# Two transformer blocks on one core: the first weight block behind each adaLN norm multiplies rows not yet normed

## What is computed

```python
def rms_norm(x, g):
    return x * lax.rsqrt(jnp.mean(x * x, -1, keepdims=True) + EPS) * g
def modulate(x, m, i):                  # shift m[3i], scale m[3i+1], gate m[3i+2]
    return x * (1 + scale) + shift
m = jax.nn.silu(cond) @ w_mod + b_mod   # 9 * 1024 numbers for LAT and for CTX, per layer
for l in range(2):
    u = modulate(rms_norm(x, g0), m, 0)                      # norm n0_l
    x = x + 0.5 * m[2] * swiglu(u, ffn_w_in[l,0], ffn_w_out[l,0])     # up_l0, down_l0
    u = modulate(rms_norm(x, g1), m, 1)                      # norm n1_l
    p = u @ w_in[l]                                          # q_l, k_l, f_l, v_l, gates
    x = x + m[5] * (mixer(p) @ w_o[l])                       # w_o_l
    u = modulate(rms_norm(x, g2), m, 2)                      # norm n2_l
    x = x + 0.5 * m[8] * swiglu(u, ffn_w_in[l,1], ffn_w_out[l,1])     # up_l1, down_l1
```

## Time and profile before

| what | value |
|---|---|
| median of 3 runs | 2754.08 us (2753.29 to 2756.24) |
| the profiled execution, its own time | 2759.6 us |
| its span | 2757.8 us |
| mean granted PE clock | 0.978 of full |
| busy: PE, DVE, ACT, POOL | 96%, 51%, 37%, 48% |
| time in weight matmuls at L1615, share of the chain that ended last | 57% |

### The profile page before, as it was taken

The page is one execution under the profiler, slowest core; times in us unless marked ns, Lnnn a source line. Parts: engine busy times, 40 slices in busy tenths (PEclk is TensorE's granted clock), DMA queues, the critical chain, the costliest instruction groups (busy, mean ns, idle before and its releaser), DMA issues.

```text
span 2757.8 us, 42480 instructions
## 1 busy us (share of the span) xinstructions
PE 2634.6 (96%) x15112; PEld 2268.3 (82%) x15112; DVE 1395.3 (51%) x3037; ACT 1023.9 (37%) x1747; POOL 1312.6 (48%) x654
## 2 busy tenths in 40 slices
PE   7998989979999999999999999999999999998997
PEld 7968989978888878867787888878888878887997
DVE  3562765675544442355497444454455453647222
ACT  4345457442322132166513232232321232463542
POOL 4505858744443434133343444444443453455875
PEclk9999989989999999999999999999999999999999
DMA  5604635554443443121243443444443453324554
GB/s 191 222 24 154 213 121 184 176 159 153 148 136 112 125 148 122 39 85 46 77 148 128 144 144 113 120 130 156 137 132 115 148 169 100 100 93 138 168 164 124
DMA packets 413994, 365.71 MB, mean 133 GB/s; under 512 B 7484, under 2 KB 412558, under 8 KB 413888
## 3 DMA queue, kind: packets, MB, share of 16 engines
q1 hardware_dynamic: 411448, 359.14, 41.0%
q10 hardware_dynamic: 2440, 5.16, 0.5%
HBM read 363.19 MB, written 1.08 MB: 132 GB/s over the span
## 4 chain that ended last, share of the span: by engine, by line
PE 68%; issue 14%; POOL 12%; DVE 3%; ACT 2%; DMA 0%; POOLq 0%; SPq 0%; ACTq 0%; DVEq 0%
PE bank L1615 57%; POOL w_lo L655 12%; PE bank L2021 2%; PE bank L1675 1%; PE bank L1676 1%; PE bank L1680 1%; PE bank L2061 1%; PE bank L1625 1%; PE bank L1966 1%; DVE stat L1521 1%; PE bank L1767 1%; PE bank L1958 1%; PE bank L2047 0%; PE bank L1978 0%; DVE bank L1145 0%
## 5 line engine op out<-in xcount | busy, mean ns | idle before, releaser
L655 POOL TENSOR_TENSOR w_lo<-raw,w_hi 128x1024 fp32r<-128x1024 f32 (+2 forms) x602 | 1285.9, 2150 | 1343.9 <-ACT w_hi L726 936.2
L1615 PE MATMUL bank<-u_hi,w_hi 128*128 128x512 f32 (+1 forms) x2488 | 854.0, 343 | 2.8 <-POOL w_lo L655 2.8
L1615 PE MATMUL bank<-u_hi,w_lo 128*128 128x512 f32 (+1 forms) x2488 | 845.9, 340 | 0.0
L1615 PE MATMUL bank<-u_lo,w_hi 128*128 128x512 f32 (+1 forms) x2488 | 845.2, 340 | 0.0
L726 ACT ACTIVATE w_hi<-raw 128x1024 fp32r<-128x1024 f32 (+3 forms) x412 | 387.0, 954 | 985.7 <-PE bank L1615 794.3
L1615 PEld LDWEIGHTS bank<-u_hi,w_hi 128*128 128x128 f32 x2488 | 473.5, 190 | 74.8 <-issue 25.1
L1615 PEld LDWEIGHTS bank<-u_hi,w_lo 128*128 128x128 f32 x2488 | 473.6, 190 | 52.7
L1615 PEld LDWEIGHTS bank<-u_lo,w_hi 128*128 128x128 f32 x2488 | 473.7, 190 | 49.1
L1189 DVE SCALAR_TENSOR_TENSOR bank<-mod_raw,cond,bank 128x256 f32<-128x256 f32 x864 | 344.7, 481 | 1.4 <-DMA mod_raw<-in_w_mod 1.4
L1615 PE MATMUL bank<-hid_hi,w_hi 128*128 128x512 f32 (+1 forms) x880 | 309.8, 352 | 11.3 <-POOL w_lo L655 11.3
L1615 PE MATMUL bank<-hid_hi,w_lo 128*128 128x512 f32 (+1 forms) x880 | 307.0, 349 | 0.0
(11 more groups left out here) (239 smaller groups left out, 3387.2 us busy)
## 6 DMA issues: line engine op xcount, KB each, us to landing
raw<-in_ffn_w_in SPq DMA_DIRECT2D x88, 1024.0 KB, 5.1
mod_raw<-in_w_mod SPq DMA_DIRECT2D x144, 512.0 KB, 4.3
raw<-in_w_in SPq DMA_DIRECT2D x67, 1024.0 KB, 5.2
raw<-in_ffn_w_out SPq DMA_DIRECT2D x64, 704.0 KB, 4.6
raw<-in_w_ffn_up SPq DMA_DIRECT2D x22, 1024.0 KB, 5.1
raw<-in_w_ffn_down SPq DMA_DIRECT2D x16, 704.0 KB, 4.8
raw<-in_w_attn_out SPq DMA_DIRECT2D x8, 1024.0 KB, 5.2
raw<-in_w_o SPq DMA_DIRECT2D x8, 1024.0 KB, 5.2
```

The source lines that it names most:

```text
L655: pool.tensor_tensor(st.half(t, w_lo[slot]), st.half(t, raw[slot]), st.half(t, w_hi[slot]).bitcast(f32), ALU.subtract).then_inc(lo_ready, 1)
L1615: ins = pe.matmul(dst, s, v, start=first and n == 0, stop=final and n == 2)
```

## The change

- Each adaLN norm becomes a `late_norm`. The first weight block behind it (`n_late` = 1; for `n0_0` the first two) multiplies "early" rows x·mod_a, not divided by the root and without the shift. ACT makes their `u_hi` (`early_tiles`) and DVE their `u_lo` (`early_rest`) in the product ahead, as each tile of x is finished; for `n0_0`, CTX between the bodies of `down1` and LAT inside `n_ffn_post`.
- PE first multiplies the block with the shift itself, in two parts (`shifts`: 2 tiles x 8 k x 2 parts = 32 matmuls of 4 columns), then runs the block (`late_blocks`). The column sums come after its k = 0, the spread after k = 1 (k = 2 where it is 256 rows wide). ACT copies the result out, DVE multiplies it by the spread root (`scale`), ACT adds W·shift as a bias (`finish`).
- Meanwhile DVE and ACT form the normed rows, which overwrite `u_hi` and `u_lo` as PE frees each k (`u_free`). The second block runs k by k as they get ready, as the first did.
- ACT splits block 2 of the product between its passes, and `split_first` puts each weight split of the product ahead before the early tiles. `root` now takes the last tile too, and `column_sums` reads it alone (4 columns instead of 8).
- The 72 pairs of `w_mod` are dealt out anew: `down_00` and `down_01` carry two pairs per body (loads after blocks 1 and 3), `gates1_2` one, and body 0 of the four up products and of `q_0`, all of `w_o_0`, `q_1` and `f_1` none. `modulation(l, 2)` moves ahead of `w_o`, `modulation(0, 0)` between the bodies of `down1`; each makes `shift_parts` besides (one copy, one subtraction).

```diff
-        gemm(f"up_{l}0", pairs(a["ffn_w_in_2"][l, 0]), 22, mod=True, banks=(0, 1))
+        first = late_norm(f"n0_{l}", 1 if l else 2, early=KD if l else 2 * KD, summed=l > 0)
+        gemm(f"up_{l}0", pairs(a["ffn_w_in_2"][l, 0]), 22, mod=1, mod_bodies=range(1, 11), banks=(0, 1), **first)
         gemm(f"down_{l}0", down(a["ffn_w_out_2"][l, 0]), 16, per=4, kt=DOWN_KT, cols=P, banks=(0, 1),
-             mod=True, acc=2)
-        norm(f"n1_{l}", TO_U, summed=True, halves=2)
-        gemm(f"q_{l}", cols(w, 0), 4, mod=True)
-        gemm(f"k_{l}", cols(w, 1024), 4, mod=True)
+             mod=1 if last else 2, acc=2, whole=True)
+        first = late_norm(f"n1_{l}", 1, passes=2 * KD // halves)
+        gemm(f"q_{l}", cols(w, 0), 4, mod=0 if last else 1, mod_bodies=range(1, 2), **first)
+        gemm(f"k_{l}", cols(w, 1024), 4, mod=1)
         gemm(f"f_{l}", cols(w, 3072), 2, gpb=halves, banks=(0, 2) if last else (0, 1, 2, 3),
-             mod=True, token_major=True)
+             mod=0 if last else 1, token_major=True)
...
         plan.add(f"att_{l}", b3=units, unit=units, o=KD)
-        gemm(f"attn_out_{l}", cols(a["w_attn_out_2"][l], 0), 4, mod=not last, counted=False)
-        gemm(f"w_o_{l}", cols(a["w_o_2"][l], 0), 4, mod=not last, acc=4)
-        norm(f"n2_{l}", TO_U, summed=True, halves=halves)
-        gemm(f"up_{l}1", pairs(a["ffn_w_in_2"][l, 1]), 22, mod=not last, banks=(0, 1))
+        gemm(f"attn_out_{l}", cols(a["w_attn_out_2"][l], 0), 4, mod=0 if last else 1, counted=False)
+        gemm(f"w_o_{l}", cols(a["w_o_2"][l], 0), 4, acc=4, whole=True)
+        first = late_norm(f"n2_{l}", 1, halves=halves)
+        gemm(f"up_{l}1", pairs(a["ffn_w_in_2"][l, 1]), 22, mod=0 if last else 1, mod_bodies=range(1, 11),
+             banks=(0, 1), **first)
         gemm(f"down_{l}1", down(a["ffn_w_out_2"][l, 1]), 16, per=4, kt=DOWN_KT, cols=P, banks=(0, 1),
-             mod=not last, acc=2)
+             mod=0 if last else 2, acc=2, whole=not last)
...
+            def late_first(name, late_tile, func, w_sums, first=0, n_sums=1, extra=None, busy=None, evac=None):
...
+                def take(st, t):
+                    act.wait_ge(group_done, st.done(0, t + 1))
+                    if busy is not None:
+                        act.wait_ge(hid_prod, busy)
+                    dst = late_tile(t)
+                    act.activation(dst, bank[t][:, 0:S * len(late_halves(name))], ACT.Copy).then_inc(late_copied, 1)
+                def finish(t):
+                    act.wait_ge(scaled, sc0 + t + 1)
+                    dst = late_tile(t)
+                    for h in late_halves(name):
+                        ins = act.activation(dst[:, in_gemm(name, h)], dst[:, in_gemm(name, h)], func, bias=shift[:, t, h:h + 1])
+                    ins.then_inc(taken[t], 1)
+                def hi(st, n):
+                    k, halves = passes[n]
+                    act.wait_ge(xn_ready, x0 + sum(len(hs) for _, hs in passes[:n + 1]))
+                    if k < KD - 1:
+                        act.wait_ge(u_free, f0 + k + 1)
+                    else:
+                        act.wait_ge(group_done, st.done(0, 2 * st.n_late))
+                    for h in halves:
+                        ins = act.activation(u_hi[:, k, h * S:(h + 1) * S], normed(n)[:, in_norm(name, h)], ACT.Identity,
+                                             bias=mod[:, 3 * i_mod * KD + k, h:h + 1])
                     ins.then_inc(u_part, 1)
+                def emit(st, pick_table):
+                    mean_root(name, w_sums, n_sums, first)
+                    if extra is not None:
+                        extra()
+                    pick_table()
+                    if st.n_late == 2:
+                        for t in range(2):
+                            split_half(st, 0, t)
+                            take(st, t)
+                        for t in range(2):
+                            finish(t)
+                        for n in range(KD):
+                            hi(st, n)
+                        for t in range(2):
+                            split_half(st, 1, t)
+                            take(st, 2 + t)
+                        return
+                    for n in range(len(passes)):
+                        hi(st, n)
+                        if n in (3, 4):
+                            split_half(st, 0, n - 3)
+                        if n == 4:
+                            take(st, 0)
+                            take(st, 1)
+                        if n in (6, 7):
+                            finish(n - 6)
+                        if n == KD + 2:
+                            for t in range(2):
+                                split_half(st, 1, t)
+                    if len(passes) == KD:
+                        for t in range(2):
+                            split_half(st, 1, t)
+                    if evac is not None:
+                        for t in range(2, 4):
+                            evac(st, t)
...
+            def early_context():
+                act.wait_ge(gains_ready, 1)
+                for k in range(KD):
+                    early_tile(k, 0, [CTX])
+            gemm("down1", between=early_context)
             mean_root("n_ffn_post", S, 1)
+            act.wait_ge(diag_ready, plan.at("n0_0", "diag"))
+            act.activation(rms[:, 0, 0:S // P], ctx_rms[:, :], ACT.Copy).then_inc(ctx_ready, 1)
+            for k in range(KD):
+                act.wait_ge(updated, KD + k + 1)
+                early_tile(k, 0, [LAT])
+                act.activation(sq[:, k, :], x[:, k, S:T], ACT.Square).then_inc(sq_ready, 1)
...
+                gemm(f"up_{l}0", silu_tiles(T, base), table=ACT.Silu,
+                     first=late_first(f"n0_{l}", late_work(T), ACT.Silu, *sums, busy=base))
+                gemm(f"down_{l}0", early_tiles(f"n1_{l}", 2), split_first=True)
...
+            def early_rest(at, i, halves):
+                for h in halves:
+                    cols = slice(h * S, (h + 1) * S)
+                    by = mod_a[:, i, at, h:h + 1] if isinstance(at, int) else mod_a[:, i, at, h]
+                    ins = dve.scalar_tensor_tensor(u_lo[:, at, cols], x[:, at, cols], by, u_hi[:, at, cols].bitcast(f32),
+                                                   ALU.mult, ALU.subtract)
+                ins.then_inc(early_lo, 1)
...
+                def take_shift():
+                    dve.wait_ge(shift_done, plan.at(name, "shift") + st.n_late)
+                    tiles = bank[2][:, 0:8 * st.n_late].rearrange("p (t c) -> p t c", c=4)
+                    n_tiles = 2 * st.n_late
+                    dve.tensor_copy(shift[:, 0:n_tiles, :], tiles[:, :, 0:2]).then_inc(dve_step, 1)
+                    steps[0] += 1
+                    dve.wait_ge(dve_step, steps[0])
+                    dve.tensor_tensor(shift[:, 0:n_tiles, :], tiles[:, :, 2:4], shift[:, 0:n_tiles, :], ALU.add) \
+                       .then_inc(taken[2], 1)
+                    dve.wait_ge(taken[2], plan.at(name, "b2") + 1)
+                def scale(t):
+                    hs = late_halves(name)
+                    cols = slice(in_norm(name, hs[0]).start, in_norm(name, hs[-1]).stop)
+                    w = cols.stop - cols.start
+                    dve.wait_ge(late_copied, plan.at(name, "scaled") + t + 1)
+                    dst = late_tile(t)
+                    dve.tensor_tensor(dst, dst, bank[5][:, cols], ALU.mult).then_inc(scaled, 1)
...
+                dve.reciprocal(rms[:, 1, 0:nt], rms[:, 0, 0:nt]).then_inc(diag_ready, 1)
+                take_shift()
+                dve.wait_ge(bcast_done, plan.at(name, "bc") + 1)
+                if st.n_late == 2:
+                    scale(0)
+                    scale(1)
+                for n in range(len(passes) + 1):
+                    if n < len(passes):
+                        norm(n)
+                    if n >= 1:
+                        rest(n - 1)
+                    if n in (6, 7) and st.n_late == 1:
+                        scale(n - 6)
...
+                    if len(pairs) == 2:
+                        for m, pair in enumerate(pairs):
+                            mod_products(pair)
+                            evac(st, i, tiles=[m], **final)
+                            take_mod(st, i, m)
+                        return
...
+                        if nxt is not None:
+                            dve.wait_ge(early_hi, i * tiles_per + (plan.at(nxt, "early") + t + 1))
+                            early_rest(at, int(nxt[1]), late_halves(nxt))
...
+            def early_context():
+                modulation(0, 0)
+                for k in range(KD):
+                    dve.wait_ge(early_hi, plan.at("n0_0", "early") + k + 1)
+                    early_rest(k, 0, [CTX])
+            def early_latent(k):
+                dve.wait_ge(early_hi, plan.at("n0_0", "early") + KD + k + 1)
+                early_rest(k, 0, [LAT])
+            clear_sums()
```

(67 more changed lines are left out.)

405 lines of the change are left out of this document (255 added, 150 removed).

## The result

The changed kernel took **2760.75 us** in the median (2755.98 to 2763.98, 12 runs) against 2753.91 (12 runs) for the kernel before; the ratio is 1.002 [1.0011, 1.0028]. By the ratio it is slower by 5.5 us (3 to 8), by the medians themselves by 6.8, where I had forecast 2.9 less. A second set gave 1.0018 [1.0009, 1.0027]. The profiled execution took 2761.9 us, its span is 2760.1.

The account below looks back on a forecast made before the run. PE was taken as the bound where most norms stand, each norm losing 9 to 9.5 us beyond its block. Terms -2.6 - 2.3 - 1.1 - 5.4 + 1.0 + 6.0 + 1.5 = -2.9 gave 2751.2 us, range 2740 to 2763.

Parts of the forecast that it names:

- the clock at the ordinary norms: Late block behind the shift run: lowered clock mostly hidden by PE's wait at G + 7.6, 0.3 us left, end G + 17.7.
- The spread: At n1_0, reciprocal behind DVE's early rests: spread ends G + 9.2 (bounds 7.9 and 12), G being the end of the product ahead.
- n0_0: Norm behind down1: later down1 end, cold second shift run and late blocks cost +6.0 us (bounds 0 and +9).
- Pairs of w_mod: Redealt modulation: eight more in down bodies +3.5, five taken away -2.2, gates1_2 +0.2; +1.5 us.
- n2_1: Norm whose last addition to root is late beside POOL's subtractions: +1.0 us (bounds -3 and +4).
- The base: Whole kernel: -2.9 us on the profiled execution of 2759.6, which lies 5.5 above the median.
- 9 + 16 x 1.4 + 1: At n1_1, k_1 waits for all 16 passes of DVE and ACT: 32.3 us against 37.6, so -5.4.
- Rival 1: Shift runs: four-column matmuls do hold the clock, or ACT gets n0_0's gains before 570; 2744.3 us, together chance 0.28.
- Rival 2: Second block at most norms: ACT's queue starves it, 2.4 us at each of four norms; 2760.8 us, chance 0.19.
- Rival 3: PE waits at the spread instead; n1_0, n0_1, n2_0 gain nothing, n1_1 keeps its gain; 2757.2 us, chance 0.15.
- the three signs by which I would be wrong: Second shift run 3.5 us; block 2 over 12 us at most norms; PE standing over 4 us ahead of the spread.

Follow-up runs that it names:

- e2_wide: Changed kernel with each shift matmul 128 columns wide (the four repeated 32 times) instead of 4; 2748.77 us, ratio 0.9984 to the kernel before.
- e1_after: The changed kernel run again unchanged, giving its second profiled execution; 2760.27 us, ratio 1.0018 to the kernel before.
- e6_gate_bank: Changed kernel with 128-column shift matmuls, CTX early tiles behind down1, and n0_0's scaled gate tiles kept in their PSUM bank; 2747.63 us, ratio 0.9969.
- e11_before: The kernel before run once more, unchanged, for its profile alone; span 2756.1 us.

## Why the prediction was wrong, point by point

- **Failed: the clock at the ordinary norms**, "PE waits at 7.6 anyway, so only 0.3 is left". I saw that a run of narrow matmuls is a danger to the clock, and then hid its price under a wait of 1.6 us that I had also computed. At n1_0 and n0_1 that wait didn't exist: PE was busy 1.00 throughout. At full clock (e2_wide) it was 0.4 us. The price is the distance above that of e2_wide: 2.6 and 4.2 us at n1_0, 2.2 at n2_0, 1.0 at n0_1, 1.6 at n1_1. I had 0.3 for each, 1.2 in all; it is 7.4 in the first execution and 9.0 in the second. The distances of the table hold the modulate of body 0, 0.44 us, before the change and not after it, which the prediction counts with the pairs; without it the changes are n1_0 -1.0 and +0.6 (forecast -2.6), n2_0 +0.5 (-1.1), n0_1 -2.0 (-2.3), n1_1 -3.4 (-5.4).
- **Wrong the other way, by less: the spread.** I had it end at G + 9.2 behind DVE's early rests. At full clock (e2_wide) it ended at G + 8.7 and the late block at G + 16.9 (G = 975.95, block 2 from 992.84), not 17.7. DVE's slowed instructions are there (2.73, 2.88 us), and cost PE those 0.4 us.
- **n0_0: forecast +6.0, measured +6.0 and +9.8.** The first is right by accident of its parts. From its first matmul to its last, down1 took 5.7 us longer (4.7 forecast), for the reason given: ACT's early tiles run at 571.53, behind the modulation, and the splits at 574.74. The norm started only 2.1 us later (86.0 instead of 83.9 us from down1's start; 88.3 in e1_after), not 6, since part of the path before had been POOL's and ACT's. The second shift run took 6.62 (7.0 forecast), the first late block 17.6 with its sums (17.2 forecast). Body 0 ended 1.4 later (122.6 instead of 121.2), where I had 6.0. What I left out comes after it, and I had put it at nothing: the four gate products of DVE, with both operands in SBUF, stand behind POOL, PE waits 2.8 us for them and does its next block in 12.62 instead of 10.9 us, at half clock behind the wait: 4.5 of the 4.6 us that are left. I knew the row that says this and applied it to `root` alone. The Trainium skill says the same ("SBUF — State Buffer", section SBUF: two separate sides: a DVE instruction with two SBUF inputs and a GpSimd instruction that reads SBUF exclude each other for their whole length); e6_gate_bank agrees, 0.88 us with one operand in PSUM while POOL subtracts.
- **Pairs of w_mod: right.** The four extra pairs per down product are +1.7 and +1.6, as worked out (3.5 for both). Of the up products three lost the pair of body 0, not four as the list of the change says: `up_11` carried none before either, and the nine of the sum have it right.
- **n2_1: forecast +1.0, measured +0.8 and +0.7**, if all of the tail is put down to it: the tail is longer by 0.4 and 0.2, and holds one modulate (f_1, 0.44) less. Right in sign and nearly in size.
- **The base.** My sum was made against the profiled execution, which had a late down1 (507.7). That was harmless for a difference. A slip in it was small: 9 + 16 x 1.4 + 1 is 32.4, so n1_1 had -5.2 and not -5.4 by its own terms.
- **Rival 1** had the right lever and the wrong sign: it said that four columns hold the clock. They didn't at any of the 16 places; 128 did at 16 of 20, and e2_wide came to 2748.8 where the rival gave 2744.3 for that case. The trace rows of one-column runs were good evidence; the rule of the Trainium skill ("TensorE: Matmul & The Clock Gate", Part 1: The HAM clock gate), read as busy time, is contradicted again by n1_0. **Rival 2** didn't happen: the second block ran back to back (1003.58 to 1014.46 at n1_0, 10.9 us). **Rival 3** neither: at the four norms PE never stood ahead of the spread. So none of the three signs by which I would be wrong came (the second shift run took 6.62 us), and the forecast failed all the same, through the clock, for which I had named no sign.

Summed from the start of down1 with the first pair: +6.0 + 1.7 - 1.4 - 0.5 + 0.0 + 1.6 - 2.5 - 0.1 - 3.4 + 0.4 = +1.8 (1.9 unrounded); with e11_before and e1_after +7.4; of the 5.5 more, 3.8 are in down1 and n0_0, where the clock fell inside the first shift run and stayed at half for longer behind the gate products, and 1.6 at n1_0. What decides the draw was not tried.

## What to carry to other kernels

When a change takes a wait away from PE, it also takes the cover off PE's clock: half clock cost the kernel before 0.8 us at n1_0, because its block waited for DVE, and cost the changed one 2.6 and 4.2 us there. Here a run of narrow matmuls could be widened from 4 to 128 columns at no cost in time (0.11 us from start to start in both, weight loads busy 1.00), and this alone turned +5.5 us into -6 in the medians of one set. And before a sum is made against one profile, look how far a stretch of the same code moves between two executions (here 7 us in 500).

## What was not expected of the hardware

- A shift run of 32 matmuls took 3.6 us with 4 columns and 3.6 us with 128, at the same start to start of 0.11 us; the clock fell behind or inside the first at n1_0 in each of 4 executions and behind the second in none of 5, PE busy 1.00 in both.
- With the same code, the half-clock time at n1_0 was 6.8 us in one execution and 10.2 in another, and the time to down1 was 501.4 and 508.1 us.
- With most of the shift run left out (e3_few_shift) the clock fell as well, now behind idle time: 3.4 us at n1_0, behind 2.2 us of idle.
